# Routed experts of a two-part transformer stack on one core: one dense expert instead of two, the first gather behind the routing, and the last block's rows returned by a one-hot product

## The reference

```python
def moe_ffn(h, w_router, b_router, w_gate, w_up, w_down):      # h: 256 x 1024, 16 experts, hidden 256
    scores = sigmoid(h @ w_router); biased = scores + b_router
    grouped = biased.reshape(256, 4, 4)                        # 4 groups of 4 experts
    best_group = argmax(sum(top_k(grouped, 2)))                # each token takes one group
    expert_idx = best_group * 4 + top_k(in_group, 2)           # and 2 of its 4 experts
    gate = normalised scores at expert_idx, else 0             # 256 x 16
    hid = silu(einsum('td,edf->tef', h, w_gate)) * einsum('td,edf->tef', h, w_up)
    return einsum('tef,efd->td', hid * gate[:, :, None], w_down)
# around it:  x = layer_norm(alpha * x + (1 + g_f) * y)
```

## Time and profile before

| | us |
|---|---|
| median of 3 runs | 1570.09 |
| the three runs | 1566.1, 1570.09, 1571.29 |
| the profiled execution | 1570.95 |
| its span (first to last instruction) | 1569.2 |
| PE busy in it | 1515.1 |
| DVE busy | 1032.3 |
| ACT busy | 703.5 |
| mean granted clock of PE | 0.991 |

### The profile page before, as it was taken

The page is one execution under the profiler, slowest core; times in us unless marked ns, Lnnn a source line. Parts: engine busy times, 40 slices in busy tenths (PEclk is TensorE's granted clock), DMA queues, the critical chain, the costliest instruction groups (busy, mean ns, idle before and its releaser), DMA issues.

```text
span 1569.2 us, 18093 instructions
## 1 busy us (share of the span) xinstructions
PE 1515.1 (97%) x6703; PEld 1082.7 (69%) x6703; DVE 1032.3 (66%) x1753; ACT 703.5 (45%) x1113; POOL 62.0 (4%) x96
## 2 busy tenths in 40 slices
PE   6999999999999999999999899999999999999998
PEld 5565657666644655676665777788887887788876
DVE  8688688876446876887662758754448659645546
ACT  1133245554311333455552468543447666534355
POOL 0010102111000000020000000000000000000000
PEclk9999899999999999999999999999999999999999
DMA  9877677999955565699996531445654821465450
GB/s 356 304 274 259 232 265 242 378 381 378 370 182 203 214 220 202 225 304 382 378 377 229 182 136 55 161 161 174 208 194 137 268 77 54 164 208 192 161 201 27
DMA packets 239095, 357.70 MB, mean 228 GB/s; under 512 B 24420, under 2 KB 166172, under 8 KB 238752
## 3 DMA queue, kind: packets, MB, share of 16 engines
q1 hardware_dynamic: 228512, 323.34, 59.6%
q0 software_dynamic: 8368, 27.83, 4.9%
q10 hardware_dynamic: 2128, 5.38, 0.9%
HBM read 345.49 MB, written 11.03 MB: 227 GB/s over the span
## 4 chain that ended last, share of the span: by engine, by line
PE 82%; DVE 9%; ACT 3%; DMA 3%; issue 2%; SPq 1%; DVEq 0%; ACTq 0%
PE psum L670 13%; PE psum L672 13%; PE psum L671 13%; PE psum L606 9%; PE psum L1216 9%; PE psum L1069 2%; DVE gring_parts L1590 2%; PE psum L677 2%; DMA gring<-in_w_up 2%; PE psum L1420 2%; PE psum L626 1%; PE psum L628 1%; PE psum L627 1%; PE psum L1396 1%; PE psum L1387 1%
## 5 line engine op out<-in xcount | busy, mean ns | idle before, releaser
L1590 DVE TENSOR_TENSOR gring_parts<-gring,arena_parts 128x2048 fp32r<-128x2048 f32 (+1 forms) x141 | 317.4, 2273 | 102.2 <-ACT arena_parts L2765 102.0
L672 PE MATMUL psum<-arena_parts,hT_parts 128*128 128x512 f32 x736 | 290.5, 395 | 0.0
L2765 ACT ACTIVATE arena_parts<-gring 128x2048 fp32r<-128x2048 f32 (+1 forms) x141 | 264.2, 1902 | 42.7 <-DMA gring<-in_w_up 42.2
L606 PE MATMUL psum<-gring,hT 128*128 128x512 f32 x384 | 178.2, 615 | 0.1
L671 PE MATMUL psum<-gring_parts,arena_parts 128*128 128x512 f32 x416 | 164.1, 394 | 0.0
L672 PEld LDWEIGHTS psum<-arena_parts,hT_parts 128*128 128x128 f32 x736 | 138.1, 188 | 33.5
L670 PE MATMUL psum<-arena_parts 128*128 128x512 f32 x384 | 152.2, 396 | 0.6 <-DVE gring_parts L1590 0.6
L670 PE MATMUL psum<-arena_parts,o_cat_parts 128*128 128x512 f32 x352 | 143.6, 408 | 0.0
L671 PE MATMUL psum<-gring_parts,o_cat_parts 128*128 128x512 f32 x352 | 138.4, 393 | 0.0
L606 PEld LDWEIGHTS psum<-gring,hT 128*128 128x128 f32 x384 | 73.1, 197 | 83.3 <-issue 82.5
L2765 ACT ACTIVATE arena<-psum 128x512 f32<-128x512 f32 (+2 forms) x96 | 52.3, 547 | 170.1 <-PE psum L606 80.4
(11 more groups left out here) (325 smaller groups left out, 2599.7 us busy)
## 6 DMA issues: line engine op xcount, KB each, us to landing
gring<-in_w_ffn_in SPq DMA_DIRECT2D x44, 1024.0 KB, 8.8
gring<-in_w_gate SPq DMA_DIRECT2D x40, 1024.0 KB, 11.5
gring<-in_w_up SPq DMA_DIRECT2D x40, 1024.0 KB, 13.9
gring<-in_w_in SPq DMA_DIRECT2D x16, 2048.0 KB, 12.3
gring<-in_w_ada SPq DMA_DIRECT2D x12, 2048.0 KB, 8.5
dring<-in_w_ffn_out SPq DMA_DIRECT2D x22, 1024.0 KB, 5.0
dring<-in_w_down SPq DMA_DIRECT2D x18, 1024.0 KB, 13.3
arena<-in_w_down SPq DMA_DIRECT2D x18, 1024.0 KB, 13.2
```

The costliest lines, as they stand in the source:

```text
L606: last = nc.tensor.matmul(ps[:, 0:n], hT[:, k, t * P:(t + 1) * P], w[:, k, 0:n], start=k == 0, stop=k == KT - 1)
L672: return nc.tensor.matmul(ps, lo, w, start=False, stop=stop)
L1590: return nc.vector.tensor_tensor(o, a, b, op)
L2765: return nc.scalar.activation(o, a, ACT.Copy)
```

## The change

- `DENSE` is 1: expert 1 becomes a unit on block 0, whose units are now 1, 2 and 3. There are 2 dense gate/up products and 19 units.
- On PE expert 1's two dense products and `dense_down(1, t)`, `dense_tr(1, t)` go. The scores are transposed after one of tile 1's eight steps; four steps follow, then `ranks`, then the last three, then the gather, and then unit 1 by `first_unit`, whose upper and lower halves wait for the upper and lower half of the gathered rows.
- DVE's routing is put in another order, interleaved with the gathered rows' scaling; new are `last_slots` (a one-hot matrix of block 4's slots, token by slot) and `slots_of` (its transposed, after PE's two transpositions). Expert 0's gate is applied in unit 2.
- Block 4's output is no longer written to DRAM: ACT rounds it (`y_hi`), DVE takes the rest (`y_lo`), and `joined(t)` multiplies both by `slots_of`. Rows of block 4 in `slots_y` are zeros, written once near the start from a zeroed buffer (DVE memset, a 512 KB DMA on POOL's queue; SP waits for it before it loads over the buffer).
- POOL's gather from `slots_y` waits for unit 16's down product and block 3's write, and lands in unit 16's slot of down weights.
- `PIECES`: the two pieces of unit 2 move, in layer 0 to units 5 and 16, in layer 1 to units 3 and 16.
- The `DF` ring starts with unit 1's down weights, so unit 5's are loaded in the loop; the dense down weights are 1 MB instead of 2 MB.

```diff
-DENSE = 2
-BLOCKS = [(2, 3)] + [tuple(range(b * EG, b * EG + EG)) for b in range(1, NG + 1)]
+DENSE = 1
+BLOCKS = [(1, 2, 3)] + [tuple(range(b * EG, b * EG + EG)) for b in range(1, NG + 1)]
...
 PIECES = (
-    {2: 2, 3: 2, 4: 3, 5: 1, 6: 2, 7: 3, 8: 2, 9: 1, 10: 3, 11: 2, 12: 2, 13: 1, 14: 3, 15: 3, 16: 2},
-    {2: 2, 3: 1, 4: 2, 5: 1, 6: 1, 7: 1, 8: 1, 9: 1, 10: 1, 11: 1, 12: 1, 13: 1, 14: 1, 15: 1},
+    {3: 2, 4: 3, 5: 2, 6: 2, 7: 3, 8: 2, 9: 1, 10: 3, 11: 2, 12: 2, 13: 1, 14: 3, 15: 3, 16: 3},
+    {3: 2, 4: 2, 5: 1, 6: 1, 7: 1, 8: 1, 9: 1, 10: 1, 11: 1, 12: 1, 13: 1, 14: 1, 15: 1, 16: 1},
...
+        y_hi, y_lo = cblock_parts[:, 1152:1152 + D], hT_parts[:, 0:D // SEQ, :].rearrange("p k n -> p (k n)")
...
-            first_half_gu(stage, 1, range(4, 8))
+            first_half_gu(stage, 1, range(4, 5))
             pe.wait_ge(scalar_done, A.at(T, "router"))
...
-            first_half_gu(stage, 1, range(4)).then_inc(tensor_done, T.step(("gu", 0)))
+            first_half_gu(stage, 1, (5, 6, 7, 0))
...
+                for t in range(TT):
+                    last = nc.tensor.transpose(ps[:, P + t * P:P + (t + 1) * P], last_slots[:, t * P:(t + 1) * P], ident)
...
+            def first_unit(n):
+                pe.wait_ge(vector_done, V.at(T, ("up read", 0, 1)))
+                for half in (1, 0):
+                    pe.wait_ge(vector_done, V.at(T, ("hg0", "parts", 0, half)))
+                    last = gate_up(psum[:, n % 2, :], n, 0, range(4 * half, 4 * half + 4), 4)
...
             def joined(t):
                 pe.wait_ge(y_gathered[t], 16 * (l + 1))
+                yg = f_slots[DF.slot(stage, "dn16")]
                 for h in range(2):
-                    last = nc.tensor.matmul(psum[:, 4 + 2 * t + h, :], ident, yg[:, t, h * N:(h + 1) * N], start=False, stop=True)
+                    nc.tensor.matmul(psum[:, 4 + 2 * t + h, :], ident, yg[:, t, h * N:(h + 1) * N], start=False, stop=False)
+                for h in range(2):
+                    pe.wait_ge(vector_done, V.at(T, ("out", LAST, h)))
+                    for y in (y_hi, y_lo):
+                        last = nc.tensor.matmul(psum[:, 4 + 2 * t + h, :], slots_of[:, t * P:(t + 1) * P], y[:, h * N:(h + 1) * N], start=False, stop=y is y_lo)
...
-            gate_up(psum[:, 0, :], 1, 0).then_inc(tensor_done, T.step(("gu0", 1)))
+            first_half_gu(stage, 1, (1, 2, 3)).then_inc(tensor_done, T.step(("gu", 0)))
             first_features()
-            gate_up(psum[:, 1, :], 1, 1).then_inc(tensor_done, T.step(("gu", 1)))
+            first_unit(DENSE)
...
             unit_tr(NU - 1)
-            dense_tr(1, 0)
             unit_down(NU - 1)
-            dense_down(0, 0)
-            dense_tr(0, 1)
-            dense_down(1, 0)
-            dense_tr(1, 1)
-            dense_down(0, 1)
-            joined(0)
-            dense_down(1, 1)
+            dense_tr(0, 1)
+            dense_down(0, 0)
+            joined(0)
+            dense_down(0, 1)
             joined(1)
...
-            block_out(NB - 1)
+            for h in range(2):
+                n = slice(h * N, (h + 1) * N)
+                dve.wait_ge(scalar_done, A.at(V, ("y hi", h)))
+                tt(y_lo[:, n], psum[:, 6 - 2 * (LAST % 2) + h, :], y_hi[:, n], ALU.subtract).then_inc(vector_done, V.step(("out", LAST, h)))
...
+            nc.vector.memset(rows[:, 1, :], 0.0).then_inc(vector_done, V.step("zeros"))
...
-            pool.wait_ge(y_written, 16 * NB * (l + 1))
+            pool.wait_ge(tensor_done, T.at(Q, ("dn", 16)))
+            if l == 0:
+                pool.wait_ge(zeros_written, 16)
+            pool.wait_ge(y_written, 16 * LAST * (l + 1))
```

143 lines of the change are left out of this document (76 added, 67 removed).

## The result

The changed kernel took 1554.17 us (median of 5 runs, 1548.53 to 1556.39), the kernel before, in runs beside them, 1566.24 (1563.97 to 1571.29): a ratio of 0.9918 with a 95% interval of 0.9899 to 0.9937, 12.8 us or 9.9 to 15.8 of gain. Run again beside the later experiments it gave 0.993 (0.9909 to 0.9952). The forecast was 1559.2, which is 0.9925 of the execution that it started from (1570.95). The profiled execution of the changed kernel took 1552.11 us.

What follows compares the result with a forecast made beforehand. PE was taken to bound the kernel, with DMA engines as full in the experts' loops. Layer 0's 6.1 (0.5 - 0.5 + 6.1) and layer 1's 5.7 (0.5 + 5.2) made 11.8 us, from 1570.95 to 1559.2; range 1553.5 to 1566.

Steps and rivals of the forecast that it cites:

- The head: Start of each layer's experts: earlier scores and gather, new PE idle of 1.3 us; 0.5 us gained per layer.
- The loop: Experts' loop: loads moved into it lose 0.5 us in layer 0 (bounds 3.5 lost, 1.9 won), 0 in layer 1.
- The tail: End of each layer's experts: residual earlier, 6.1 us gained in layer 0; 5.2 in layer 1, limited by the small parameters.
- The sum: Both layers: 6.1 us in layer 0 and 5.7 in layer 1, 11.8 together, taken from the profiled execution of 1570.95.
- The loads decide: Rival, both layers' loops: the 1.05 MB and the moved piece cost 3.0 and 3.5 us more, 1565.7; 15%.
- Longer handovers: Rival, in the head between PE, ACT and DVE: 1.5 us more idle per layer, 1562.2; 10%.
- Slower: Rival, unit 1's wait for the gathered rows' upper half: rows come no earlier, 6.7 us more idle per layer, 1576; 4%.
- More than the sum: Rival: layer 0's late stalls go, the piece costs nothing, the second stage's pause shortens; 3.0 to 5.0 us better, 1555; 12%.
- the piece: Layer 0's loop: 0.26 MB of loads moved from unit 2 to late in the loop, 0.7 us of DMA.
- At the start: Start of the kernel: the 128x1024 memset on DVE is hidden, at most 0.3 us outside.

Runs made afterwards that it cites:

- again: The changed kernel, unchanged, run and profiled once more in a later series: ratio 0.9930 (0.9909 to 0.9952) to the kernel before.
- the copy: Changed kernel with one more DMA per layer, copying 1 MB from DRAM to DRAM behind unit 10: ratio 0.9951 to the kernel before.
- the late gather: Changed kernel with the gather from `slots_y` issued behind unit 19's down product instead of unit 16's: ratio 0.9948 to the kernel before.

## Why the prediction was right, and where not

**The head: right.** Forecast 0.5 gained per layer and an idle of 1.3; measured 0.62 in layer 0 (unit 4 starts 45.51 behind R0 instead of 46.13), 0.67 in layer 1, and an idle of 1.29 in both. Nothing waits for block 1's rows. Putting the scores back where they stood costs 1.67 at the gather's start. The chain ACT, ACT, DVE behind the gather's upper half took 3.04 us; 2.9 was summed.

**The loop: this step failed.** "I take -0.5 in layer 0": the loads moved into the loop were to lose 0.5, and it was 0.8 gained, an error of 1.3. The stalls of 0.75, 0.80 and 1.92 became 0.17, 0.81 and 1.88. The run with the last block through DRAM, whose loop is the same but for the gather, needs from R0 to T 207.67 us where the changed kernel needs 207.71 and the kernel before 209.14, so the gain is there twice; by "again" it is 0.1, or up to 1.8 without its half-clock stretch. The size is open, but a loss is in none of them: the 1.05 MB fewer loaded ahead cost nothing. That the head frees slots earlier would explain it; no run tried that apart, nor the moved pieces. In layer 1 0 was forecast, and nothing was lost or gained beyond 0.1. That bytes cost time there is true (2.0 us for 1 MB moved twice, none in layer 1), but none came on top. And the stalls of the earlier trace rows were not the loads' alone, as the prediction had it: with the copies moved ahead both went, while ACT's wait stayed. PE needed copies that stood behind an ACT instruction waiting for weights wanted 5 us later.

**The tail: right in both layers.** Forecast T + 6.52 for the residual, measured T + 6.49; gain 6.17 against 6.1. The one-hot products cost 0.23 each, as the split products of the same shape and type, not 0.86, so the term that the prediction took from its nearest row holds. In layer 1 the joined products end 5.46 nearer to T (5.2 forecast), and P comes 5.66 nearer: the limit was the parameters, which PE still waited 1.06 for. What I hadn't seen is how the gain is made. I priced PE's removed work (7.2) and the trip apart, and the runs show that they don't add: removing the dense expert without the one-hot path gave nothing in the timed runs and 4.2 in the trace, for the trip through DRAM, covered in the kernel before, then stands open with 1.60 and 3.17 us of idle and a halved clock behind it.

**The sum and its base: the step that cost most.** 11.8 was forecast; by the pair of traces it was 13.9 (1.3 of the 2.1 are the loop's, the rest 0.1 to 0.5 in each head and tail), by the timed runs 12.8 (9.9 to 15.8). The predicted time of 1559.2 was 5.0 us too high mostly for another reason: "From the profiled one". That execution, 1570.95, had the three half-clock stretches before R0, 17 us at half the clock or 8.5 us of time, of which the prediction took no account. The median of the five runs beside the changed kernel is 1566.24, and from it the same sum gives 1554.4, where 1554.17 was measured. The range hung on the same base, so its lower end, 1553.5, stood too high as well: the measured ratio times 1566.24 is 1553.4. The median of three runs that the prediction had, 1570.09, would have helped by 0.9 only; that it agreed with the profiled execution was chance, for 25 later runs of the same kernel have a median of 1564.81. That 11.8 lies so near the timed 12.8 is in part luck: the runs' interval holds 13.9 as well.

**The rivals.** "The loads decide" is out by the copy, "Longer handovers" by the idle of 1.29. "Slower" had its place right, for the rows come when PE waits for them, and its condition never came. Of "More than the sum" the stall of 1.9 stayed (1.88), the piece did cost nothing, and the pause was shorter (2.94 instead of 3.71), but not for the clock: the window behind the tail reads 0.93 in both kernels. Over all twelve profiles the idle of 1.29 in the head had no half-clock stretch behind it in any of its 15 places; the one of 1.66 had one in layer 0 and none in layer 1; the one of 1.87 to 1.97 at unit 16 had one in four profiles of six; the one behind layer 1's tail (1.55 to 5.92) in eleven of twelve; and the one of 3.82 in layer 0's tail, in the run through DRAM, had one as well. The Trainium skill, "TensorE: Matmul & The Clock Gate", "HAM oscillation - how this bites in real kernels", shows a loop whose waits for DMA of about 3 to 5 us each leave the next burst cold. The waits of 3.17 and 5.92 us here agree. But here some of 1.55 to 1.97 had it too, and the new pause of 1.3, which the prediction feared by that section, never.

**At the start.** The memset took 0.91 us, and the first product with c began at 4.68 instead of 4.67: hidden.

## What to carry to other kernels

Work that covers a transfer has two prices: its own, and that of what it covers. In the timed runs taking only the work or only the transfer away gave 0.0 and -2.8 us here, both together 12.8; so price the pair, and look for the next wait after each. Where an in-order engine waits for a load that is wanted later, look at what small copies stand behind it. And forecast a gain apart from the time it is taken from: a median of three and one profiled execution were 3.9 and 4.7 us above the median of five. Look at the profiled execution's clock for what it lost by chance, and compare stretches between fixed instructions.

## What was not expected of the hardware

Executions of one program differ by up to 13.5 us (1551.22 to 1564.71 in ten runs of the late gather; 1561.6 to 1569.84 in 25 of the kernel before). Between profiled executions a good part is how many stretches at a granted clock of 0.5 (1.2 GHz) they have. All twelve profiles have one to three of them, 3.41 or 6.83 us long, between 146 and 195 us, where PE is busy for 58 to 59 of 60 us in the three windows above, and one or two more between 554 and 591 us, in the next layer's mixing part. Two have one of 10.24 us at 1292.65 and 1297.17, for 3.1 us each, and the other ten none. What brings these on in busy stretches stays open.

POOL took 1.7 to 3.1 us for an indirect DMA in 31 places of the twelve profiles, each time across one of DVE's products of two 128x2048 tensors, and about 0.97 elsewhere. Others that also lay across such a product stayed at 0.97, and the starts tell them apart. In the changed kernel, layer 0, POOL and DVE:

```profile
407.59 0.98 POOL L3641 DMA_INDIRECT arena<-slots_y,dest  x1 [17.89 <-DMA slots_y<-cblock]
408.88 2.22 POOL L3641 DMA_INDIRECT arena<-slots_y,dest  x1 [0.31 <-issue]
407.96 2.29 DVE L1601 TENSOR_TENSOR gring_parts<-gring,arena_parts 128x2048 fp32r<-128x2048 f32 x1 [0.41 <-ACT arena_parts L2778]
```

The first starts before DVE's product and takes 0.98; the second starts within it and ends at 411.10, 0.85 us behind the product's end. So it is everywhere: the 34 that started at least 0.03 us into such a product all ended 0.83 to 0.90 us behind its end, and those that started before it, or within 0.02 us of its start, took 0.96 to 1.00. POOL's plain DMAs, which read no indices, are not held: 250 of them started within such a product and took 0.53 to 0.58 or 0.79 to 0.80 us, as outside. In the Trainium skill, "GPSIMD Engine Reference", "Specifications", the engine shares its SBUF interfaces with VectorE, with contention where a DVE instruction has two SBUF inputs. The trace agrees for the indirect DMAs. No run moved a DMA or a product to try it.
